# Norm factors from full-width ones products with a logarithm, an exponential and a Newton step, in place of per-token column sums, a GpSimd power and a spread

## The reference, cut to what matters

```
rmsnorm(x, g) = x * rsqrt(mean(x*x) + 1e-6) * g
x += 0.5 * rmsnorm(SwiGLU_1(rmsnorm(x)))
x +=       rmsnorm(Mixer(rmsnorm(x)))
x += 0.5 * rmsnorm(SwiGLU_2(rmsnorm(x)))
```

## Time and profile before

| | |
|---|---|
| runs, median (lowest to highest) | 2229.8 us (2228.38 to 2230.82), 3 runs |
| the profiled execution's own time | 2230.11 us |
| its span, first to last instruction | 2228.3 us |
| busy: PE, DVE, ACT, POOL | 99%, 61%, 53%, 34% |
| share of the chain that ended last | PE 93%, DVE 3%, POOL 2%, issue 2% |
| mean granted TensorE clock | 0.997 |

### The profile page before, as it was taken

The page is one execution under the profiler, slowest core; times in us unless marked ns, Lnnn a source line. Parts: engine busy times, 40 slices in busy tenths (PEclk is TensorE's granted clock), DMA queues, the critical chain, the costliest instruction groups (busy, mean ns, idle before and its releaser), DMA issues.

```text
span 2228.3 us, 40420 instructions
## 1 busy us (share of the span) xinstructions
PE 2207.4 (99%) x16870; PEld 2183.1 (98%) x16870; DVE 1360.4 (61%) x1771; ACT 1177.6 (53%) x1832; POOL 753.6 (34%) x802
## 2 busy tenths in 40 slices
PE   8999999999999999999999999999999999999998
PEld 8999999999999999999999999999999999999998
DVE  6555757657785557745574557576578756475454
ACT  6534547536675445543454355574467654464443
POOL 4012512516545225521251124134264533252112
PEclk9999999999999999999999999999999999999999
DMA  6555555445544455555555555554454444655553
GB/s 225 167 161 163 167 167 157 143 122 164 160 143 138 130 175 157 166 165 163 163 165 164 162 164 161 167 161 133 127 178 151 143 133 131 182 162 159 163 165 129
DMA packets 102405, 350.62 MB, mean 157 GB/s; under 512 B 11440, under 2 KB 16560, under 8 KB 102224
## 3 DMA queue, kind: packets, MB, share of 16 engines
q1 hardware_dynamic: 100992, 346.76, 51.3%
q10 hardware_dynamic: 1232, 1.27, 0.2%
HBM read 343.12 MB, written 4.87 MB: 156 GB/s over the span
## 4 chain that ended last, share of the span: by engine, by line
PE 93%; DVE 3%; POOL 2%; issue 2%; ACT 0%; DMA 0%; SPq 0%; DVEq 0%; POOLq 0%
PE psD L447 87%; DVE wl L1051 1%; POOL ssum L1470 1%; PE psS L453 1%; PE psM L589 1%; DVE hl L1103 1%; PE psM L565 1%; DVE y L1089 0%; DVE x L1093 0%; PE psM L671 0%; PE psM L642 0%; PE psM L648 0%; DMA x<-in_xT 0%; PE psM L595 0%; PE psS L491 0%
## 5 line engine op out<-in xcount | busy, mean ns | idle before, releaser
L447 PE MATMUL psD<-hh,wh 128*128 128x288 f32 x3712 | 1109.4, 299 | 4.9 <-DVE hl L1103 3.1
L447 PE MATMUL psD<-hl,wh 128*128 128x288 f32 x3712 | 1096.7, 295 | 0.0
L447 PE MATMUL psD<-hh,wl 128*128 128x288 f32 x3712 | 1093.5, 295 | 0.0
L1051 DVE TENSOR_TENSOR wl<-raw,wh 128x1024 fp32r<-128x1024 f32 (+1 forms) x656 | 818.7, 1249 | 133.4 <-ACT wh L759 133.3
L759 ACT ACTIVATE wh<-raw 128x1024 fp32r<-128x1024 f32 (+1 forms) x656 | 672.5, 1027 | 104.8 <-DMA raw<-in_w_gu 52.5
L447 PEld LDWEIGHTS psD<-hh,wh 128*128 128x128 f32 x3712 | 697.6, 188 | 11.4 <-issue 6.1
L447 PEld LDWEIGHTS psD<-hh,wl 128*128 128x128 f32 x3712 | 700.6, 189 | 0.0
L447 PEld LDWEIGHTS psD<-hl,wh 128*128 128x128 f32 x3712 | 698.9, 188 | 0.9
L1707 POOL TENSOR_TENSOR hidl<-hid,hidh 128x288 fp32r<-128x288 f32 x176 | 210.1, 1194 | 930.7 <-ACT hidh L1001 930.7
L447 PE MATMUL psD<-hidh,wh 128*128 128x288 f32 x1408 | 417.5, 296 | 0.0
L447 PE MATMUL psD<-hidl,wh 128*128 128x288 f32 x1408 | 415.5, 295 | 0.0
(11 more groups left out here) (192 smaller groups left out, 1460.4 us busy)
## 6 DMA issues: line engine op xcount, KB each, us to landing
raw<-in_w_gu SPq DMA_DIRECT2D x352, 512.0 KB, 3.6
raw<-in_w_d SPq DMA_DIRECT2D x128, 448.0 KB, 3.2
raw<-in_w_in SPq DMA_DIRECT2D x80, 512.0 KB, 3.6
raw<-in_w_d SPq DMA_DIRECT2D x64, 512.0 KB, 3.6
raw<-in_w_out SPq DMA_DIRECT2D x32, 512.0 KB, 3.6
gates<-in_w_ax SPq DMA_DIRECT2D x4, 512.0 KB, 4.5
S<-in_st_gla SPq DMA_DIRECT2D x4, 512.0 KB, 4.6
out_gla_s<-S SPq DMA_DIRECT2D x4, 512.0 KB, 5.6
```

Source lines behind the costliest of these rows:

```text
L447: mm = e.matmul(out, w[:, kt * P:(kt + 1) * P], t[:, kt, :], start=(kt == 0 and part == 0), stop=(kt == KT - 1 and part == 2))
L1051: e.tensor_tensor(wl[u % RING][:, 0:width], raw[u % RING][:, 0:width], wh[u % RING][:, 0:width].bitcast(F32), ALU.subtract).then_inc(lo_re ...
```

## The change

Column sums, POOL's power, diagonals and spreads go. PE multiplies `ssum` by a matrix of ones, which leaves the token's sum on all 128 partitions at once: as one fp32 product at quick places, otherwise as two float32r products of a split (`ssh` by ACT, `ssl` by DVE). ACT takes Ln and Exp(-0.5 ...) of it as a first guess (with a preload of the table set `natural_log_exp_and_others` each time), DVE makes a Newton step of three operations, and the factor lies in SBUF, where `rescale` reads it; `keep_rstd` and its copy go. The boundary (st 1, g0), wout g0 to the next stage, becomes quick. At the mixer's end the lru sum is taken at slot 29 instead of 15, the outputs are squared as they leave PSUM, ACT and DVE split 1440 columns (slots 30 and 31), PE makes ten float32r products at slot 33, ACT's roots come at slots 34 and 35, DVE's nine Newton operations at 35 and 36, the values one slot later than before.

```diff
-T_LRU_SUM = 15
-T_VALUES = T_SUMS + 5
+T_LRU_SUM = 29
+T_VALUES = T_SUMS + 6
     def is_quick(l, st, g):
-        return (st, g) == (0, 1) or is_final(l, st)
+        return (st, g) in ((0, 1), (1, 0)) or is_final(l, st)
...
# tensor
-                columns(ssum[g], True, True).then_inc(cols_ready, 1)
+            elif quick:
+                e.wait_ge(sq_used[g], (DT - 1) * (group_event[g] + 1))
+                e.matmul(out, ones[:, :].bitcast(F32), ssum[g][:, :], start=True, stop=True).then_inc(sums_done, 1)
+            else:
+                splits[0] += 1
+                e.wait_ge(ssl_ready, splits[0])
+                e.matmul(out, ones[:, :], ssh[g][:, :], start=True, stop=False)
+                e.matmul(out, ones[:, :], ssl[g][:, :], start=False, stop=True).then_inc(sums_done, 1)
...
-                if slot == T_SUMS + 4:
-                    spread_one()
-                    e.wait_ge(s_ready, 3 * i + 3)
-                for h in range(HEADS):
-                    if slot == T_SUMS + 4 + (h + 1) // 2:
-                        spread(psM[:, h, 0:T])
+                if slot == T_SUMS + 2:
+                    sums_free()
+                    e.wait_ge(stl_ready, i + 1)
+                    e.wait_ge(s_ready, 3 * i + 3)
+                    for k in range(STATS):
+                        out = psM[:, k - 1, 0:T] if k else psS[:, 0, 0:T]
+                        e.matmul(out, ones[:, :], sth5[g][:, k, :], start=True, stop=False)
+                        mm = e.matmul(out, ones[:, :], stl5[g][:, k, :], start=False, stop=True)
+                    mm.then_inc(sums_done, 1)
...
# scalar
+        def first_guess(g, floored=False, keep=False):
+            event[0] += 1
+            if event[0] - mixers[0] > 1:
+                e.wait_ge(factor_ready, event[0] - mixers[0] - 1)
+            e.preload_act_table_set("natural_log_exp_and_others")
+            if floored:
+                e.wait_ge(stat_read, event[0])
+                ln = steps.mark(e.activation(guess[:, :], factor[:, :], ACT.Ln))
             else:
+                e.wait_ge(sums_done, event[0])
+                ln = steps.mark(e.activation(guess[:, :], psS[:, 0, 0:T], ACT.Ln, scale=1.0 / D, bias=epsc[:, :]))
+            if keep:
+                e.activation(floor[g][:, :], psS[:, 0, 0:T], ACT.Identity, scale=EPS / D, bias=eps2c[:, :])
+            steps.after(ln)
+            e.activation(guess[:, :], guess[:, :], ACT.Exp, scale=-0.5).then_inc(guess_ready, 1)
...
+                if slot == T_SUMS + 3:
+                    e.preload_act_table_set("natural_log_exp_and_others")
+                    e.activation(guess5[g][:, 0, :], psS[:, 0, 0:T], ACT.Ln, scale=1.0 / DL, bias=epsc[:, :])
+                    ln = steps.mark(e.activation(guess5[g][:, 1:3, :], psM[:, 0:2, 0:T], ACT.Ln, scale=1.0 / DV, bias=epsc[:, :]))
+                    steps.after(ln)
+                    e.activation(guess5[g][:, 0:3, :], guess5[g][:, 0:3, :], ACT.Exp, scale=-0.5).then_inc(guess5_ready, 1)
+                if slot == T_SUMS + 4:
+                    e.preload_act_table_set("natural_log_exp_and_others")
+                    ln = steps.mark(e.activation(guess5[g][:, 3:5, :], psM[:, 2:4, 0:T], ACT.Ln, scale=1.0 / DV, bias=epsc[:, :]))
...
# vector
+        def newton(out, floored=False):
...
+                e.scalar_tensor_tensor(factor[:, :], psS[:, 0, 0:T], D * EPS, guess[:, :], ALU.add, ALU.mult).then_inc(stat_read, 1)
+                e.wait_ge(stat_read, event[0])
+            steps.mark(e.scalar_tensor_tensor(factor[:, :], factor[:, :], -0.5 if floored else -0.5 / D, guess[:, :], ALU.mult, ALU.mult))
+            steps.after()
+            e.scalar_tensor_tensor(out[:, :], factor[:, :], 1.5, guess[:, :], ALU.add, ALU.mult).then_inc(factor_ready, 1)
...
-            e.tensor_tensor(tiles, tiles, psS[:, 0, 0:T].unsqueeze(1).broadcast_to([P, n, T]), ALU.mult).then_inc(y_normed[g], 1)
+            e.tensor_tensor(tiles, tiles, factor[:, :].unsqueeze(1).broadcast_to([P, n, T]), ALU.mult).then_inc(y_normed[g], 1)
```

More of the change, by code:

```diff
@@ L200, in program @@
     ssum = [sb(f"ssum{g}", [P, T]) for g in range(G)]
[L201 to L208, removed]
+    sq, sq_at = [], []
+    for g in range(G):
+        sq_at.append(cursor[0])
+        sq.append([sb(f"sq{g}{s}", [P, T]) for s in range(2)])
+    guess = sb("guess", [P, T])
+    factor = sb("factor", [P, T])
+    floor = [sb(f"floor{g}", [P, T]) for g in range(G)]
     par = sb("par", [P, L * NPAR])
@@ L242, in program @@
     qf = sb("qf", [P, PR, NSL - 2, C])
+    ssh, ssl = [], []
+    for g in range(G):
+        cursor[0] = sq_at[g]
+        ssh.append(sb(f"ssh{g}", [P, T], F32R))
+        ssl.append(sb(f"ssl{g}", [P, T], F32R))
     dec, kf, vt, ket, kem = [], [], [], [], []
+    sth5, stl5, guess5, factor5 = [], [], [], []
     for g in range(G):
@@ L449, in unit @@
             mm.then_inc(unit_done, 1)
[L451 to L455, removed]
         def sums_free():
-            if last_use:
-                e.wait_ge(*last_use[-1])
-        def token_sums(g, normed=None, final=False):
+            if event[0]:
+                e.wait_ge(stat_read, event[0])
@@ L825, in boundary @@
             first = start + (3 if is_quick(l, st, g) else 4)
-            for slot in range(end + 1):
-                if slot == start:
-                    token_sums(g, st != 1)
+            quick = is_quick(l, st, g)
+            for slot in range(end + 2):
+                if slot in (start, end) and not quick:
+                    split_sums(g)
+                if slot == (start if quick else start + 1):
+                    first_guess(g, floored=st != 1)
                     if final:
@@ L836, in boundary @@
                         square(g, t, x[g][:, t, :])
-                if slot == end:
-                    token_sums(g, keep=st != 0)
+                if slot == (end if quick else end + 1):
+                    first_guess(g, keep=st != 0)
                 yield
@@ L1039, in _ @@
         event = [0]
-        kept = [0]
-        spreads = [0]
-        spread_of = []
+        factors = [0]
+        splits = [0]
         lows = [0]
@@ L1122, in boundary @@
             for slot in range(end + 3):
-                if slot == start + hop - 1:
-                    token_diagonal(quick)
+                if slot in (start, end) and not quick:
+                    low_sums(g)
+                if slot == start + hop - 1 and st != 1:
+                    add_floor(g)
                 if slot == start + hop:
+                    newton(factor, floored=st != 1)
                     if st == 1:
@@ L1520, in boundary @@
             for slot in range(end + 1):
-                if slot == start:
-                    root(NTC, floor=g if st != 1 else None, quick=quick)
                 k = (slot - start - hop - 1) * at_once
@@ L1538, in boundary @@
                         add_square(g, t)
-                if slot == end:
-                    root(NTC, keep=g if st != 0 else None, quick=quick)
                 yield
```

277 lines of the change are left out of this document (100 added, 177 removed).

## The result

The changed kernel takes **2240.9 us** (median of 8 runs, 2235.5 to 2242.3) against 2231.2 for the kernel before, measured beside it in as many runs: ratio 1.0036, 95% interval 1.0027 to 1.0045. It is slower, by more than the 0.2% that can be told from nothing. The forecast was 2220, with 2206 to 2231 as its range. A second measurement, in a later group, gave 1.0043 (1.0030 to 1.0055).

A forecast was written before the change was run, and what follows sets the result against it. PE, busy 99% of the span, was taken as the bound; -6.9 - 0.6 - 1.5 + 3.4 - 4.9 + 0.25 = -10.25 us took the profiled 2230.1 to 2219.9, 2220 as a median, range 2206 to 2231.

The forecast's parts named there:

- Ordinary events: Of 17 ordinary column-sum events, 13 stay ordinary: each goes from 0.79 to 0.26 us of PE, sum -6.9 us.
- The start: Program start: the first take, waiting for the factor, comes at 22.5 and unit 3 no longer waits as long: -1.5 us.
- The mixer's end of g1: Twice: PE saves 3.0 us, but ACT and DVE queues make it wait about 3.0 for `hidl`: net +1.7 each, +3.4.
- The forecast's 1.65 each: At the mixer's end of g1, the clock was expected to drop behind PE's wait for `hidl`, costing 1.65 us more.
- From the mixer's end of g0 to the end of win g1, twice: Stretch through wout g0 into win g1: PE's savings mostly not cashed at first; net -2.45 us each, -4.9 together.
- What was queued behind DVE there then runs as before, apart from y's scaling.: At the boundary from wout g0 to win g1: work behind DVE unchanged, only y's scaling charged extra, 1.2 us a pair.
- I charge 1.2 us for the pair: y's two scalings, reading their factor from SBUF beside POOL's adds of x: 1.2 us, bounds 0 and 2.7.
- None of this is cashed at first: From the mixer's end of g0: PE's savings gain nothing before the boundary, since ACT is still 2 us late there.
- PE's wait shrinks from 2.15 to 1.5 or so: Wait for `xc` at the end of win g1: shorter, so the clock stays up, worth another -1.65 us.
- The finals: Final events: g0 -0.75 us, the tail of g1 +1.0 including 0.3 for contention; sum +0.25.
- The shared-port rival: At four mixer's ends, nine Newton operations beside POOL cost double, 6.9 us an end: +17 us, 2247; chance 0.10.
- The drain: About 1.38 us per ACT table-set switch by the skill: 4.1 us longer per mixer's end, about 2230; given little chance.

## Why the prediction was wrong

**What held.** Ordinary events: the profile shows 0.26 us of PE for each of the 13 and a step of 0.52 down at each, as the forecast's 0.53. The fp32 product at a quick place without a wait costs 0.47, forecast 0.48. The start gave 2.7 us for 1.5, by the times of the first and the 385th unit product; the first itself came 0.5 later, so that 2.2 are left. *The mixer's end of g1* is nearly as written: side products 4.28 to 1.33 (forecast 4.3 to 1.3), a wait of 3.1 beyond the usual distance for the last `hidl` (forecast 3.0), in both layers. Only the clock did as it liked:

```profile
787.99 0.29 PE L458 MATMUL psD<-hidl,wh 128*128 128x288 f32 x1
788.12 0.29 PE L458 MATMUL psD<-hidh,wl 128*128 128x288 f32 x1
791.39 0.61 PE L458 MATMUL psD<-hidh,wh 128*128 128x288 f32 x1 [2.97 <-POOL hidl L1660]
...
792.04 0.44 PE L458 MATMUL psD<-hidh,wl 128*128 128x288 f32 x1
```

Behind this wait the products stand 0.24 us apart, the lower level of 1.2 GHz, for 6.8 us in layer 0; behind the same wait at 1894.65 in layer 1, and behind both in the second profile of the same kernel, they do not. The forecast's 1.65 each is the mean of 3.4 and 0 in the one profile, which is luck.

**The step that failed** is "From the mixer's end of g0 to the end of win g1, twice": forecast -2.45 each and -0.3 for the quick event, -5.5 in all. Measured by the time of the same unit products before and after, the stretch costs +4.8 us in layer 0 and +7.7 in layer 1 (+3.8 and +6.3 in the profile with fewer falls of the clock). Against the forecast that is 18.0 of the 22.5 us in the one profile and 15.6 of the 15.7 in the other. Four sentences of that step are wrong:

- "What was queued behind DVE there then runs as before, apart from y's scaling." The forecast saw that the 32 values move into the shared port, said so in its sentence on the rule, and put no term for them into the sum. They take 0.35 us more each on average, 1.5 to 2.05 instead of 0.93 for the two of a slot at the end of g0. They are worth 7.9 us by the medians.
- "I charge 1.2 us for the pair" of scalings. It charged DVE at one boundary. The price fell on POOL, whose adds feed the same chain, and on the two final events, where DVE alternates with POOL: 11.8 us for the whole kernel by the medians, against 2.4 in the sum and 0.3 at the tail.
- "None of this is cashed at first", with PE ahead and only 2 us late. Nothing in it followed POOL's list. The values stand one slot later, so that two adds of squares stand behind the last low part, and the quick product of ffn g1's end, which had waited for nothing, waits 2.4 us from start to start in each layer. No edit tried took that away with profit.
- "PE's wait shrinks from 2.15 to 1.5 or so", with the clock staying up. From start to start the wait for `xc` at the end of win g1 went from 2.44 to 2.62 in layer 0 and from 2.44 to 2.61 in layer 1. The clock stayed up behind it in one of the two layers of the first profile and in none of the second: this -1.65 came once in four times, by luck.

**The finals** were +0.25 and came to +1.2 at g0 and +2.4 at the tail. Both are the price of the scalings again: with those out of PSUM the first is -0.7, the -0.75 of the forecast, by the unit products at 2000 and 2036 of the kernel before, and the tail is +0.8, for the +0.7 that the forecast had without contention.

**The shared-port rival** had the right mechanism and the right sign, at the wrong place and size. It put the contention on the nine Newton operations and asked for 6.9 us an end. Three of the nine read PSUM, so that by the rule it went by only six could contend, and those hardly do: of three of 576 columns only the second, beside a `hidl`, takes 1.02 in place of 0.76, since POOL is idle beside the others, as the earlier trace rows had it. Its chance of 0.10 was too low, because it was priced only where POOL was seen to be idle, and the places where POOL was seen to be busy (the values, the adds of x, the tail) were left to a charge of 1.2.

**The drain** that the Trainium skill (ScalarE: Activation LUTs, What ACT_TABLE_LOAD costs) adds to each switch of sets shows in no trace here: at the mixer's ends of the changed kernel Ln starts 0.02 us after the load's 1.28. The estimate of 4.1 us also counted three switches, where the second load brings the set that is there already. The run that left a load out left out that one, so it tests the price of a load, not of a switch.

## What to carry to other kernels

When an edit moves an operand from PSUM to SBUF, list every VectorE operation that now reads two SBUF inputs, look which GpSimd operations run at those times, and price both engines: an unchanged duration on the one says nothing if the other came second. Writing the result of a short chain back into PSUM, where its sums were, costs no instruction, only a later wait for the bank, and was worth 19 us here by the medians and 15 by the fastest runs.

Count a saving on the bounding engine, then walk the list of every engine that it will now reach earlier. Here PE saved 24 us and met lists of DVE and POOL that its side products had hidden before. Taking a table load away brought nothing while three operations on DVE stood in front; moving these by two slots as well brought 5.9 us.

## What the hardware showed that I had not expected

- An operation with two SBUF inputs on DVE and one on POOL exclude each other for about the whole of the first: POOL's 0.81 us became 2.01 beside a scaling of 1.35, while the scaling kept its 1.35. Which of the two shows the time depends on which comes second: at the tail it was DVE's add, 1.84 for 0.76.
- The same waits of PE, 2.4 to 3.3 us long, are followed by a fall of the clock in one execution and by none in another, and some falls follow small products without a wait. The fourteen runs of the changed kernel spread, along with their mean clock, from 2235.5 to 2242.3: four near 2235.6 (mean clock 0.993 or 0.994), seven near 2242 (0.990), three between. A difference of 7 us between two kernels with such waits can be this alone; runs of both, in number, are needed.
